# Two convolved up-projections: high and low token parts in one 512-wide matmul, halves summed by VectorE, part of the weight split on GpSimd

## The reference

```python
def causal_dwconv(x, w, b):            # K = 3 taps along the tokens, each channel by itself
    ...
def conv_ffn(h, w_in, conv_w, conv_b, w_out):
    z = causal_dwconv(h @ w_in, conv_w, conv_b)
    u, g = jnp.split(z, 2, axis=-1)
    return (jax.nn.gelu(g) * u) @ w_out
```

## Time and profile before

| | |
|---|---|
| time, median of 3 runs | 1724.5 us (1720.9 to 1725.56) |
| span of the profiled execution | 1723.2 us |
| its own time | not listed apart from the three runs |
| TensorE, share of the span with a matmul in flight | 99% |
| VectorE, ScalarE, GpSimd busy | 80%, 58%, 2% |
| TensorE's granted clock, mean | 0.998 of full speed |
| matmuls of `f0_up`, slabs 2 to 21 | from 118.52 us to 233.7 us |
| HBM traffic | 212 GB/s over the span |

### The profile page before, as it was taken

How to read it: one execution, slowest core, us unless ns; L and a number is a source line. 1 busy time by engine, 2 the same in 40 slices (tenths; PEclk the granted TensorE clock), 3 DMA queues, 4 the chain that set the end, 5 groups by cost and what they waited for, 6 DMA issues and landing times.

```text
span 1723.2 us, 29149 instructions
## 1 busy us (share of the span) xinstructions
PE 1700.8 (99%) x11414; PEld 1540.2 (89%) x11414; DVE 1385.6 (80%) x2193; ACT 993.5 (58%) x1578; POOL 26.5 (2%) x37
## 2 busy tenths in 40 slices
PE   8999999999999999999999899999999999999999
PEld 8799998999998988889998698888888888798888
DVE  5778888888888888899986879888988876866654
ACT  6565545766554555446677756553655456865542
POOL 0300000000000000000000100000000000000000
PEclk9999999999999999999999999999999999999999
DMA  9245468444547777795442057779677845035552
GB/s 373 98 171 196 172 219 317 181 162 172 195 171 277 278 286 280 277 358 185 180 174 98 25 196 262 273 282 345 259 277 280 313 168 189 25 147 195 193 178 93
DMA packets 62436, 367.06 MB, mean 213 GB/s; under 512 B 6944, under 2 KB 7328, under 8 KB 27776
## 3 DMA queue, kind: packets, MB, share of 16 engines
q1 hardware_dynamic: 61776, 362.70, 57.2%
q0 software_dynamic: 560, 3.01, 0.4%
HBM read 364.64 MB, written 1.05 MB: 212 GB/s over the span
## 4 chain that ended last, share of the span: by engine, by line
PE 88%; DVE 6%; ACT 3%; DMA 2%; issue 1%; SPq 0%; DVEq 0%; ACTq 0%
PE psum L504 17%; PE psum L525 11%; PE psum L379 11%; PE psum L381 11%; PE psum L380 11%; PE psum L506 9%; PE psum L527 6%; PE psum L432 4%; DVE lo L1868 1%; PE psum L494 1%; DMA raw<-slabs_dram 1%; PE psum L572 1%; ACT hi L1234 1%; DMA modw<-wmod_dram 1%; PE psum L497 1%
## 5 line engine op out<-in xcount | busy, mean ns | idle before, releaser
L1868 DVE TENSOR_TENSOR lo<-raw,hi 128x1024 fp32r<-128x1024 f32 x522 | 619.5, 1225 | 162.2 <-ACT hi L1234 162.1
L1234 ACT ACTIVATE hi<-raw 128x1024 fp32r<-128x1024 f32 x522 | 522.8, 1051 | 344.9 <-PE psum L527 191.5
L504 PE MATMUL psum<-XHL,hi 128*128 128x512 f32 x1280 | 452.5, 399 | 0.0
L379 PE MATMUL psum<-XHL,hi 128*128 128x256 f32 x1320 | 375.9, 285 | 1.5 <-DVE lo L1868 1.5
L380 PE MATMUL psum<-XHL,hi 128*128 128x256 f32 x1320 | 373.5, 283 | 0.0
L381 PE MATMUL psum<-XHL,lo 128*128 128x256 f32 x1320 | 373.4, 283 | 0.0
L506 PE MATMUL psum<-XHL,lo 128*128 128x256 f32 x1280 | 359.5, 281 | 0.0
L525 PE MATMUL psum<-HHL,hi 128*128 (+1 forms) x960 | 338.8, 398 | 0.4 <-DVE S L2058 0.4
L504 PEld LDWEIGHTS psum<-XHL,hi 128*128 128x128 f32 x1280 | 240.5, 188 | 59.7
L527 PE MATMUL psum<-HHL,lo 128*128 (+1 forms) x960 | 269.5, 281 | 0.0
L379 PEld LDWEIGHTS psum<-XHL,hi 128*128 128x128 f32 x1320 | 253.2, 192 | 4.3 <-issue 2.4
(11 more groups left out here) (342 smaller groups left out, 2027.6 us busy)
## 6 DMA issues: line engine op xcount, KB each, us to landing
raw<-slabs_dram SPq DMA_DIRECT2D x269, 1024.0 KB, 5.3
modw<-wmod_dram SPq DMA_DIRECT2D x144, 512.0 KB, 5.4
raw<-slabs_dram SPq DMA_DIRECT2D x4, 512.0 KB, 7.5
A<-small_dram POOLq DMA_DIRECT2D x1, 1536.0 KB, 13.7
X<-x_dram SPq DMA_DIRECT2D x4, 256.0 KB, 4.7
out_dram<-X SPq DMA_DIRECT2D x3, 256.0 KB, 2.3
cond<-cvec_dram POOLq DMA_DIRECT2D x1, 512.0 KB, 8.0
A<-tab_dram POOLq DMA_DIRECT2D x1, 512.0 KB, 15.6
```

The costliest lines, as they stand in the source:

```text
L379: mm(dst, wh, xh, start=start, stop=False, skip_group_check=True)
L504: mm(dst, hi[:, k, j * P:(j + 1) * P], XHL[:, kt, :, :].rearrange("p a t -> p (a t)"), start=start, stop=False, skip_group_check=True)
L1234: f(hi[:, k % SPLIT, at], raw[:, n % RAW, at], ACT.Copy).then_inc(q["hi_ready"], 1)
L1868: v.tensor_tensor(lo[:, k % SPLIT, at], raw[:, n % RAW, at], hi[:, k % SPLIT, at].bitcast(F32), ALU.subtract).then_inc(q["lo_ready"], 1)
```

## The change

- Both convolved up stages go through `gated_stage`, so slabs 2 to 21 use `wide` instead of `three`, and two banks per slab instead of a half-used rotation of four. `up_stage` is gone. The first slab stays 256 columns wide; the second keeps its matmuls, but puts low weights x highs and highs x token lows into the second half of its banks.
- ScalarE first copies the second halves of slab s from PSUM to `LOWS` (`keep_low`), then splits slab s+2. Its scale-and-bias activations now read `WHOLE` in SBUF and wait for VectorE's sum. The gelu of a pair comes after the activations of the next pair's first slab.
- VectorE first adds the halves into `WHOLE` (`whole`), then makes the low part of slab s+2, then does the four tap instructions with both tensor operands in SBUF; the product of a pair comes after the taps of the next pair's first slab.
- For slabs 4 to 21 of both stages (`SHARED`, 36 slabs) VectorE makes only the first half of `lo`; GpSimd makes the second (`second_halves`). TensorE waits for it before the second half of the slab, SyncE before it loads that raw buffer again.
- ScalarE's and VectorE's loops over these stages are unrolled.
- The down stages' first slab takes the order of `GATED_BANKS`.

```diff
+SHARED = {N0[_name] + _s: 18 * CONVED.index(_name) + _s - 4 for _name in CONVED for _s in range(4, 22)}
...
# SyncE, load()
                     sp.wait_ge(q["lo_ready"], 2 * (SPLITS[n - RAW] + 1))
+                    if n - RAW in SHARED:
+                        sp.wait_ge(q["lo_second"], SHARED[n - RAW] + 1)
...
# TensorE, gated_slab()
                 for m in range(2):
-                    pe.wait_ge(q["lo_ready"], plus(2 * SPLITS[n] + m + 1, i, 8))
+                    if m and n in SHARED:
+                        pe.wait_ge(q["lo_second"], plus(SHARED[n] + 1, i, 4))
+                    else:
+                        pe.wait_ge(q["lo_ready"], plus(2 * SPLITS[n] + m + 1, i, 8))
...
-            up_stage("f0_up", 3, 6)
-            ffn_down("f0_down", "f0_up", [(m, 17) for m in range(4, 8)] + [((N0["f0_up"] + s) % 4, s) for s in range(18, 22)])
+            gated_stage("f0_up", 3, 6)
...
# ScalarE, conv_ffn()
+                def keep_low(s):
+                    act.wait_ge(q["slab_used"], N0[stage] + s + 1)
+                    if s >= 2:
+                        act.wait_ge(*up_count(stage, s - 2))
+                    b = s // 2 % 2 * 4 + s % 2 * 2
+                    f(LOWS[s % 2].rearrange("p (a t) -> p a t", a=2), psum[:, b:b + 2, T:2 * T],
+                      ACT.Copy).then_inc(q["low_kept"], 1)
+                def linear(p, side):
+                    s, b = 2 * p + side, p % 2
+                    if s:
+                        act.wait_ge(*up_count(stage, s))
...
+                        last = f(S[:, b * 1024 + side * 512 + m * T:b * 1024 + side * 512 + (m + 1) * T],
+                                 WHOLE[s % 2][:, m * T:(m + 1) * T], ACT.Identity,
+                                 scale=col(f"fconv{layer}", 88 + k), bias=col(f"fconvb{layer}", k))
...
+                for s in range(22):
+                    if s:
+                        keep_low(s)
+                    split_hi(N0[stage] + s + 2)
+                    linear(s // 2, s % 2)
+                    if s % 2 == 0 and s:
+                        gelu(s // 2 - 1)
+                gelu(10)
...
# VectorE, split_lo()
+                    last.then_inc(q["lo_ready"], 2 if n in SHARED else 1)
+                    if n in SHARED:
+                        break
...
# VectorE, conv_ffn()
+                    v.tensor_tensor(two(WHOLE[s % 2]), psum[:, b:b + 2, 0:T], two(LOWS[s % 2]),
+                                    ALU.add).then_inc(evacuated[s % 2], 1)
...
-                            source = bank[n % 4]
...
+                            last = stt(out=z, in0=WHOLE[s % 2][:, m * T:(m + 1) * T - tap],
+                                       scalar=col(f"fconv{layer}", (2 - tap) * 44 + k), in1=z,
+                                       op0=ALU.mult, op1=ALU.add)
...
+                for s in range(22):
+                    whole(s)
+                    split_lo(N0[stage] + s + 2)
+                    if s == 0:
+                        dve.wait_ge(q["raw_kept"], norms[0])
+                    taps(s // 2, s % 2)
+                    if s == 0:
+                        v.memset(tiny[:, 202:203], 0.0).then_inc(evacuated[0], 1)
+                    if s % 2 == 0 and s:
+                        product(s // 2 - 1)
+                product(10)
...
# GpSimd
+            def second_halves(stage):
+                at = slice(HALF, SLAB)
+                for s in range(4, 22):
+                    n = N0[stage] + s
+                    k = SPLITS[n]
+                    pool.wait_ge(q["hi_ready"], 2 * k + 2)
+                    g.tensor_tensor(lo[:, k % SPLIT, at], raw[:, n % RAW, at],
+                                    hi[:, k % SPLIT, at].bitcast(F32), ALU.subtract).then_inc(q["lo_second"], 1)
```

More of the change, by code:

```diff
@@ L417, in ssd_slab, with raw_slab @@
                 last.then_inc(q["slab_used"], 1)
-            def raw_slab(stage, dst, wide=T, bank_of_sums=3):
+            def raw_slab(stage, dst, wide=T, bank_of_sums=3, apart=False):
                 n, k = N0[stage], norms[0]
@@ L432, in part @@
                         last = mm(dst(m), raw[:, n % RAW, at], source[:, kt, 0:wide],
-                                  start=(kt == 0 and (m == 0 or wide > T)), stop=False, skip_group_check=True)
+                                  start=(kt == 0 and (m == 0 or wide > T or apart)), stop=False, skip_group_check=True)
                     return last
@@ L585, in gated_stage @@
                 ffn_down(DOWN[stage], stage, GATED_BANKS)
[L587 to L599, removed]
             def down_slab(stage, s, i=None):
@@ L854, in _ @@
             down_stage("rg_out")
-            up_stage("f1_up", 5)
-            ffn_down("f1_down", "f1_up", [(m, 17) for m in range(4, 8)] + [((N0["f1_up"] + s) % 4, s) for s in range(18, 22)])
+            gated_stage("f1_up", 5)
             gated_stage("g00_up", 6)
@@ new lines, in keep_low @@
+                def keep_low(s):
[9 more added lines that the diff above has]
+                        act.wait_ge(*up_count(stage, s))
+                    else:
+                        raw_kept()
+                    if side == 0 and p >= 2:
+                        act.wait_ge(q["h_ready"], HID[DOWN[stage]] + p - 1)
+                    for m in range(2):
+                        k = 2 * p + m + 22 * side
+                        last = f(S[:, b * 1024 + side * 512 + m * T:b * 1024 + side * 512 + (m + 1) * T],
+                                 WHOLE[s % 2][:, m * T:(m + 1) * T], ACT.Identity,
+                                 scale=col(f"fconv{layer}", 88 + k), bias=col(f"fconvb{layer}", k))
+                    last.then_inc(q["lin_ready"], 1)
@@ L1867, in split_lo @@
                     at = slice(h * HALF, (h + 1) * HALF)
-                    v.tensor_tensor(lo[:, k % SPLIT, at], raw[:, n % RAW, at],
-                                    hi[:, k % SPLIT, at].bitcast(F32), ALU.subtract).then_inc(q["lo_ready"], 1)
+                    last = v.tensor_tensor(lo[:, k % SPLIT, at], raw[:, n % RAW, at],
+                                           hi[:, k % SPLIT, at].bitcast(F32), ALU.subtract)
+                    last.then_inc(q["lo_ready"], 2 if n in SHARED else 1)
+                    if n in SHARED:
+                        break
             def unscaled(z, banks):
@@ L2035, in hidden @@
                 v.tensor_tensor(hl, two(buf), hh.bitcast(F32), ALU.subtract).then_inc(q["h_ready"], 1)
-            def conv_ffn(stage, layer, gelus):
-                def pair(p, i=None):
-                    b = p % 2
[L2040 to L2067, removed]
@@ new lines, in conv_ffn, with whole, taps, product @@
+            def conv_ffn(stage, layer):
+                def whole(s):
+                    if s == 0:
+                        dve.wait_ge(q["slab_used"], N0[stage] + 1)
+                        unscaled(WHOLE[0], psum[:, 0:2, 0:T]).then_inc(q["raw_kept"], 1)
+                        return
+                    dve.wait_ge(q["low_kept"], 21 * layer + s)
+                    b = s // 2 % 2 * 4 + s % 2 * 2
+                    v.tensor_tensor(two(WHOLE[s % 2]), psum[:, b:b + 2, 0:T], two(LOWS[s % 2]),
+                                    ALU.add).then_inc(evacuated[s % 2], 1)
+                def taps(p, side):
+                    s = 2 * p + side
+                    dve.wait_ge(q["lin_ready"], LIN[stage] + s + 1)
+                    marks = []
+                    for tap in (1, 2):
+                        for m in range(2):
+                            k = 2 * p + m + 22 * side
+                            at = p % 2 * 1024 + side * 512 + m * T
+                            z = S[:, at + tap:at + T]
+                            if tap == 2:
+                                step.wait(marks[m])
+                            last = stt(out=z, in0=WHOLE[s % 2][:, m * T:(m + 1) * T - tap],
+                                       scalar=col(f"fconv{layer}", (2 - tap) * 44 + k), in1=z,
+                                       op0=ALU.mult, op1=ALU.add)
+                            if tap == 1:
+                                marks.append(step.put(last))
+                    last.then_inc(q["g_conved" if side else "u_conved"], 1)
+                def product(p):
+                    b = p % 2
+                    dve.wait_ge(q["gelu_ready"], 11 * layer + p + 1)
+                    dve.wait_ge(q["u_conved"], 11 * layer + p + 1)
@@ L2068, in pair @@
                     buf = S[:, 3072 + b * 512:3584 + b * 512]
-                    hidden(buf, stage, p, i, v.tensor_tensor(
+                    hidden(buf, stage, p, None, v.tensor_tensor(
                         buf, S[:, 2048 + b * 512:2560 + b * 512], S[:, b * 1024:b * 1024 + 512], ALU.mult))
[L2072 to L2079, removed]
```

46 lines of the change are left out of this document (15 added, 31 removed).

## The result

The changed kernel takes 1738.6 us (median of 4 runs, 1735.6 to 1740.9) against 1724.55 us before: ratio 1.0082, 95% interval 1.0066 to 1.0098. It is slower by 14 us, where I had forecast no change that could be measured. The profiled execution's span is 1739.1 us, 15.9 above that of before.

A forecast was written before the change was run, and what follows sets the result against it. TensorE was taken as the bound, with VectorE about to tie; -4.2 (wide matmuls) - 0.5 (down-stage waits) + 1.8 (GpSimd's turns) = -2.9 us, 1721.6 on the median 1724.5, called 1722; range 1718.5 to 1737.

The forecast's parts named there:

- What bounds, and TensorE's part: Convolved up stages: TensorE is the bound; 640 matmul triples become pairs, 0.3600 to 0.3534 us each, saving 4.2 us.
- The waits at the down stage, -0.5: `ffn_down`: TensorE's waits for late taps, 1.5 us with weight loads, shrink; 0.5 us saved, ends 0 and 1.5.
- VectorE's own 8.47 us a pair: VectorE's sums, low parts, taps and product chain per pair of slabs take 8.47 us of TensorE's 11.31.
- Turns, and what is exempt: GpSimd blocks VectorE instructions with two SBUF operands, low parts and taps; those reading one operand from PSUM pass undisturbed.
- The length of a turn, taken as 1.70: Each half shared with GpSimd costs VectorE up to 1.70 us, against the 1.14 it saves.
- the upper bound: GpSimd's turn at most 2.2 us, four times the 256-wide one's 0.55: pair 12.4 us, time +15.
- the forecast's tie: VectorE's pair 11.4 us against TensorE's 11.31, +1.8 us over 18 pairs; slabs 2 to 21 take 114; chance 0.40.
- What is hidden, 0.8 a pair: Of GpSimd's turns, 0.6 us beside VectorE's sum and 0.2 in its wait for ScalarE cost nothing, per pair.
- hand-overs of 0.2 to 0.4: Waits between engines add 0.2 to 0.4 us to VectorE's pair of slabs, giving 11.3 to 11.5.
- my formula: VectorE's pair: 8.47 us plus two turns, less 0.8 hidden, plus hand-over waits (0.3 in the upper case).
- the third: Rival: taking turns makes VectorE the bound, TensorE waits at L504; 12.1 to 12.4 us a pair, 1734 to 1740; chance 0.27.

The follow-up runs named there:

- experiment 1: Changed kernel without the sharing: VectorE makes both low halves of every slab, GpSimd idle; 1720.96 us, ratio 0.9974.
- experiment 3: Kernel before, with unused GpSimd instructions of differing operands and output types added in the last down stage; 1.89 us (one range read twice) or 2.39 each (different ranges).
- experiment 4: Changed kernel with GpSimd reading the raw weights as both operands, so the shared second low half is zero; 1723.75 us, ratio 0.9993.

## Why the prediction was wrong

- **What bounds, and TensorE's part: right.** 0.360 and 0.3534 a pair gave 113.1 us for 20 slabs; experiment 1 took 113.07. The 4.2 us are there.
- **The waits at the down stage, -0.5: wrong.** They went, but in the kernel before `f1_down` ran at the faster pace behind its short wait (0.3467 a pair) and in the changed kernel at the slower: 61.80 us before, 62.29 after. In `f0_down`, where it had not, 62.78 became 62.29. Together nothing.
- **VectorE's own 8.47 us a pair: right.** 12.13 less the 2.09 and 1.60 of the two stretched low parts is 8.44.
- **Turns, and what is exempt: right.** Low parts and taps with two SBUF operands are held up, sums and PSUM taps are not. In `f0_up` 12 of the 18 turns fell on low parts, 5 on taps and 1 on the product's low part.
- **The length of a turn, taken as 1.70: this step failed.** It is about 2.2: 2.09 with 0.2 of GpSimd's work already past, and 1.60 with 0.6 beside the sum. I chose the row of the same shape and named the output type as the only difference; the difference was that it read nearly the same range twice, as experiment 3 showed. The other row that I had, 0.55 us for a quarter of the width, scaled to 2.2, and I kept it only as the upper bound. With 1.70 in place experiment 4 gives 1723.75, close to the forecast of 1722. A part of this closeness is luck: its stages took 115.4 us where the forecast's tie was 114, and the faster pace of both down stages gave 2.2 us back in the profiled execution.
- **What is hidden, 0.8 a pair, and hand-overs of 0.2 to 0.4: too kind and too harsh.** With 2.2 my formula says 8.47 + 4.4 - 0.8 + 0.3 = 12.4 and +15 us; the pair was 12.13 and the time +14. About 0.7 was hidden (8.44 + 4.4 - 12.13), and once VectorE is late there are no hand-over waits left.
- **The rival that came true** was the third, VectorE as the bound: its 12.1 to 12.4 a pair and 1734 to 1740 us held the result. I gave it 0.27 and cut the range in the midst of it, at 1737, though the 2.2 in it was scaled from a measured row. It named L504 as the place of TensorE's wait, and that matmul, now L510, is where it waits.

## What to carry to other kernels

Before work goes from VectorE to GpSimd, list VectorE's instructions that read two SBUF operands: only beside the others does GpSimd's time come free. An edit that moves an operand from PSUM to SBUF takes instructions out of the second group, so try the two edits apart. When two engines come within a few per cent of each other, the size of one instruction decides the sign: take its price from a row with the same operands, not only the same shape, and let the range hold the scaled one.

## What the runs showed that I had not expected

- GpSimd's 1024-wide two-operand instruction takes 1.89 us when both operands are one range and 2.39 when they differ. The output type made no difference in either case (2.38 with float32r in experiment 3, 1.90 at the shortest in experiment 4).
- A stretch of the same pairs of matmuls runs at 0.3467 or 0.3533 us a pair, 2% apart, at the same granted clock, and keeps its pace over hundreds of pairs until TensorE waits. Work put into the stream did not change it (0 of 6). After a wait it was sometimes the faster: 6 of 18 in the changed kernel, 4 of 6 after the long waits, 1 of 6 after the short ones in the one profiled execution. What at the instant of the start decides is open, and so is how to get the faster pace every time; as an estimate, all six up stages at it, each with its down stage (480 pairs), would be worth 6 x 480 x 0.0067 = 19 us.
